# One level of Strassen's scheme in 21 of the 44 input-projection pairs of each layer, in a two-layer hybrid decoder step

## What is computed

```python
h = rms_norm(x, P['norm_mix'][l])
z = jnp.einsum('btd,dn->btn', h, P['w_in'][l])      # d = 1024, some 11300 columns
a_q, a_k, a_v, b_q, b_k, b_v, b_g, b_lr, c_qkv, c_z, c_b, c_a, gates = jnp.split(z, split_points(), axis=-1)
...
merged = (g_a * jnp.einsum('btc,cd->btd', o_a, wb[0]) + g_b * jnp.einsum('btc,cd->btd', o_b, wb[1])
          + g_c * jnp.einsum('btc,cd->btd', o_c, wb[2]))
out = jnp.einsum('btd,de->bte', merged, P['w_out'][l])
```

## Time and profile before

| | |
|---|---|
| Median of 3 runs | 1804.47 us (1804.31 to 1809.21) |
| Span of the profiled execution, first to last instruction | 1802.1 us |
| TensorE busy | 1748.8 us, 97% |
| VectorE busy | 743.5 us, 41% |
| ScalarE busy | 364.3 us, 20% |
| Mean granted TensorE clock | 0.993 |

### The profile page before, as it was taken

The page is one execution under the profiler, slowest core; times in us unless marked ns, Lnnn a source line. Parts: engine busy times, 40 slices in busy tenths (PEclk is TensorE's granted clock), DMA queues, the critical chain, the costliest instruction groups (busy, mean ns, idle before and its releaser), DMA issues.

```text
span 1802.1 us, 30183 instructions
## 1 busy us (share of the span) xinstructions
PE 1748.8 (97%) x12542; PEld 1282.9 (71%) x12542; DVE 743.5 (41%) x1548; ACT 364.3 (20%) x760; POOL 154.3 (9%) x259
## 2 busy tenths in 40 slices
PE   9999999999999999999999998999989999999997
PEld 7889888787768999978898887877663343333423
DVE  3444542434535765534544414355342332233222
ACT  2241333433101000012313333331011110100001
POOL 3000000403200111000100002032000000000000
PEclk9999999999999999999999999999999999999999
DMA  9833599999999997899535899899958999999994
GB/s 296 285 120 100 187 324 316 359 310 367 388 347 392 365 321 286 288 348 371 194 107 207 308 325 346 312 350 384 333 211 327 393 377 414 402 398 394 371 415 177
DMA packets 265853, 563.96 MB, mean 313 GB/s; under 512 B 14654, under 2 KB 163362, under 8 KB 265441
## 3 DMA queue, kind: packets, MB, share of 16 engines
q1 hardware_dynamic: 246384, 500.15, 76.8%
q0 software_dynamic: 18544, 58.58, 9.2%
q10 hardware_dynamic: 784, 3.26, 0.5%
HBM read 547.75 MB, written 196.63 MB: 413 GB/s over the span
## 4 chain that ended last, share of the span: by engine, by line
PE 85%; SPq 7%; DMA 4%; DVE 2%; issue 1%; ACT 1%; DVEq 0%; POOL 0%; ACTq 0%; POOLq 0%
PE PS L940 34%; PE PS L1598 8%; PE PS L1374 8%; SPq L811 7%; PE PS L1350 5%; PE PS L1382 4%; PE PS L859 3%; PE PS L986 3%; PE PS L1576 3%; PE PS L1364 2%; PE PS L979 2%; PE PS L1636 2%; PE PS L1321 1%; PE PS L1537 1%; DMA mem<-bias_tables 1%
## 5 line engine op out<-in xcount | busy, mean ns | idle before, releaser
L940 PE MATMUL PS<-h,mem 128*128 128x264 f32 x2816 | 654.3, 389 | 0.0
L940 PEld LDWEIGHTS PS<-h,mem 128*128 128x128 f32 x2816 | 527.8, 191 | 106.7 <-issue 21.3
L1806 ACT COPY z<-PS 128x264 f32<-128x264 f32 (+5 forms) x293 | 119.5, 430 | 737.6 <-PE PS L940 527.6
L1598 PE MATMUL PS<-mem,z 128*32 128x512 f32 (+1 forms) x1536 | 146.1, 523 | 3.8 <-DMA mem<-in_moe_w_up 3.8
L2893 DVE COPY small<-mem 128x1024 f32 x56 | 38.8, 693 | 175.6 <-PE PS L1576 117.8
L1598 PEld LDWEIGHTS PS<-mem,z 128*32 128x32 f32 x1536 | 47.4, 110 | 77.8 <-issue 61.2
L1576 PE MATMUL PS<-small,z 128*32 128x256 f32 (+2 forms) x624 | 86.9, 396 | 1.3 <-DVE z L2893 1.3
L1350 PE MATMUL PS<-z,mem 128*128 128x264 f32 x384 | 87.3, 388 | 0.0
L1576 PE MATMUL PS<-z 128*32 128x256 f32 (+2 forms) x624 | 87.0, 396 | 0.0
L1350 PEld LDWEIGHTS PS<-z,mem 128*128 128x128 f32 x384 | 72.3, 190 | 13.8 <-issue 1.7
L1374 PE MATMUL PS<-z,mem 128*128 128x132 f32 x624 | 78.3, 278 | 0.0
(11 more groups left out here) (377 smaller groups left out, 2028.2 us busy)
## 6 DMA issues: line engine op xcount, KB each, us to landing
out_win_s<-in_cache_win_kv SPq DMA_DIRECT2D x128, 1023.5 KB, 11.9
mem<-in_w_in SPq DMA_DIRECT2D x88, 1024.0 KB, 7.6
mem<-in_moe_w_gate SPq DMA_DIRECT2D x80, 512.0 KB, 9.7
mem<-in_moe_w_up SPq DMA_DIRECT2D x80, 512.0 KB, 8.9
mem<-in_moe_w_down SPq DMA_DIRECT2D x64, 512.0 KB, 13.6
out_win_s<-in_cache_win_kv SPq DMA_DIRECT2D x32, 1022.0 KB, 13.1
z<-in_moe_w_down SPq DMA_DIRECT2D x48, 512.0 KB, 13.1
z<-in_moe_w_up SPq DMA_DIRECT2D x32, 512.0 KB, 10.6
```

What stands on the lines that cost most here:

```text
L940: last = mm(bank(l, "p", j)[:, 0:T], w[:, k, P * (j % 2):P * (j % 2) + P], h[:, k, :], start=(k == 0), stop=(k == KT - 1))
L1598: last = mm(m_bank("c", "gu", g, b, w, r)[BLK * j:BLK * j + BLK, 0:n], hs[:, k, P * r + BLK * j:P * r + BLK * j + BLK], v3(slot_ap(set_slo ...
L1806: return nc.scalar.copy(out, in_)
```

## The change

For the 21 pairs of `FOLD` in each layer the two tiles are computed together by one level of Strassen's scheme. The weight chunk is split into quarters a11, a12, a21, a22 (4 blocks of 128 by 128 columns each), h into h11, h12, h21, h22 (4 blocks by 132 tokens). Seven products of four half-width matmuls take the place of sixteen matmuls: fold_x (a11 h11, and s2 by a sum of h), fold_y (s1, and a difference of weights), fold_x2 and fold_y2 (the rest, accumulated into the same banks, 0 for x and 1 for y). VectorE forms the weight sums in fold_w (four additions of 128 x 512), once a layer the sums of h in fold_h, and puts the products together: a reduction of fold_x, a reduction and an addition for fold_y, an addition for fold_y2. ScalarE copies fold_x2's half width instead of two tiles. fold_w of a pair stands in the list right behind fold_x of the pair before, where that is folded too, and else behind the first tile of the pair before. The fifth slot of the projection's ring becomes the place of the sums of h, so the ring has four slots (`RING, BASE = 4, 5`). The core of the diff:

```diff
-RING = 5
+RING, BASE = 4, 5
...
+HALF = T // 2
+UNSETTLED = ("proj", "fold_x", "fold_y", "fold_x2", "fold_y2", "fold_w")
+FOLD = (8, 9, 10, 11, *range(15, 20), *range(23, 32), 33, 35, 37)
...
+    def tile(j):
+        q = j // 2
+        if q not in FOLD:
+            return [("proj", j)]
+        return [("fold_x2", q), ("fold_y2", q)] if j % 2 else [("fold_x", q), ("fold_y", q)]
...
-    s += p() + [("small_turn",)] + p(2) + [("conv_v", 0)] + p() + [("gate_c",)] + p() + [("conv_v", 1)]
+    s += p() + [("small_turn",), ("fold_h",)] + p(2) + [("conv_v", 0)] + p() + [("gate_c",)] + p() + [("conv_v", 1)]
...
-        return [step, ("proj_half", j), (step[0] + "2", *step[1:]), ("proj", j)]
+        first, rest = tile(j) if j // 2 in FOLD else (("proj_half", j), ("proj", j))
+        return [step, first, (step[0] + "2", *step[1:]), rest]
...
+    for q in FOLD:
+        before = ("fold_x", q - 1) if q - 1 in FOLD else ("proj", 2 * q - 2)
+        s.insert(s.index(before) + 1, ("fold_w", q))
...
-        FIXED = dict(par=0, ab=1, xn=2)
+        FIXED = dict(par=0, ab=1, xn=2, fold_x=0, fold_x2=0, fold_y=1, fold_y2=1)
...
-                place(n0 + q, q % RING, (l, "p", 2 * q + 1))
+                place(n0 + q, q % RING, (l, "fold_y2", q) if q in FOLD else (l, "p", 2 * q + 1))
+            held[BASE - 1] = (l, "fold_y2", FOLD[-1])
...
+            def fold_x(l, q):
+                wait_chunk(pe, CH0[l] + q)
+                open_bank(pe, l, "fold_x", q)
+                x_ = bank(l, "fold_x", q)
+                four(x_[:, 0:HALF], fold_quarters(l, q)[0], h[:, 0:4, 0:HALF], True)
+                pe.wait_ge(hd_ready, h_sum(l, 3))
+                pe.wait_ge(fw_even, even_sum(l, q, 1))
+                four(x_[:, HALF:T], fold_sums(q)[1], fold_t[:, 1]).then_inc(full(l, "fold_x", q), 1)
+
+            def fold_y(l, q):
+                pe.wait_ge(fw_odd, odd_sum(l, q))
+                open_bank(pe, l, "fold_y", q)
+                y_ = bank(l, "fold_y", q)
+                four(y_[:, 0:HALF], fold_sums(q)[0], fold_t[:, 0], True)
+                four(y_[:, HALF:T], fold_quarters(l, q)[2], fold_t[:, 2]).then_inc(full(l, "fold_y", q), 1)
...
+            def fold_y2(l, q):
+                open_bank(pe, l, "fold_y2", q)
+                y_ = bank(l, "fold_y2", q)
+                four(y_[:, HALF:T], fold_quarters(l, q)[3], fold_t[:, 3])
+                pe.wait_ge(fw_even, even_sum(l, q, 2))
+                four(y_[:, 0:HALF], fold_sums(q)[2], h[:, 4:8, HALF:T]).then_inc(full(l, "fold_y2", q), 1)
...
+            def fold_w(l, q):
+                wait_chunk(dve, CH0[l] + q)
+                if fold_before(q) is not None:
+                    wait_full(dve, l, "fold_y2", fold_before(q))
...
+                a11, a12, a21, a22 = fold_quarters(l, q)
+                s1, s2, s4 = fold_sums(q)
+                tt(s1, a21, a22, ADD)
+                tt(a21, a11, a21, SUB).then_inc(fw_odd, 1)
+                dve.wait_ge(fw_odd, odd_sum(l, q))
+                tt(s2, a22, a21, SUB).then_inc(fw_even, 1)
+                dve.wait_ge(fw_even, even_sum(l, q, 1))
+                tt(s4, a12, s2, SUB).then_inc(fw_even, 1)
+
+            def fold_x(l, q):
+                if q != FOLD[0]:
+                    wait_read(dve, l, "fold_y2", FOLD[FOLD.index(q) - 1])
+                wait_full(dve, l, "fold_x", q)
+                nc.vector.tensor_reduce(fold_ve[:, 0, :], bank(l, "fold_x", q)[:, 0:T].rearrange("p (w t) -> p t w", w=2),
+                                        AX.X, ADD).then_inc(free(l, "fold_x", q), 1)
+
+            def fold_y(l, q):
+                wait_full(dve, l, "fold_y", q)
+                nc.vector.tensor_reduce(fold_ve[:, 1, :], bank(l, "fold_y", q)[:, 0:T].rearrange("p (w t) -> p t w", w=2),
+                                        AX.X, ADD).then_inc(free(l, "fold_y", q), 1)
+                wait_read(dve, l, "fold_x", q)
+                wait_read(dve, l, "fold_y", q)
+                tt(fold_out(q)[:, 3 * HALF:4 * HALF], fold_ve[:, 0, :], fold_ve[:, 1, :], ADD)
+
+            def fold_y2(l, q):
+                wait_full(dve, l, "fold_y2", q)
+                tt(v3(fold_out(q)[:, HALF:3 * HALF], 2), v3(bank(l, "fold_y2", q)[:, 0:T], 2),
+                   bc(fold_ve[:, 0, :], 1, [P, 2, HALF]), ADD).then_inc(free(l, "fold_y2", q), 1)
```

More of the change, by code:

```diff
@@ L136, in mixer_jobs @@
         return [("p", *a)]
+    if k in ("fold_x", "fold_y", "fold_x2", "fold_y2"):
+        return [(k, *a)]
     if k == "conv_s":
@@ L596, in wait_z @@
         def wait_z(eng, l, lo, hi):
-            for j in range(max(lo, hi - 2), hi):
+            for j in [j for j in range(lo, hi) if j // 2 not in FOLD][-2:]:
                 wait_read(eng, l, "p", j)
+            for q in [q for q in FOLD if lo <= 2 * q + 1 and 2 * q < hi][-1:]:
+                wait_read(eng, l, "fold_x2", q)
+                wait_read(eng, l, "fold_y2", q)
         CH0 = [0, CH_MIX + CH_FFG + CH_FFD]
@@ L950, in proj, with four, fold_x2 @@
                 proj_ks(l, j, range(4, KT) if (l, j) in halved else range(KT))
+            def four(out, left, right, opens=False):
+                for k in range(4):
+                    last = mm(out, left[:, k, :], right[:, k, :], start=(opens and k == 0), stop=(k == 3), skip_group_check=True)
+                return last
+            def fold_x(l, q):
[12 more added lines that the diff above has]
+                four(y_[:, HALF:T], fold_quarters(l, q)[2], fold_t[:, 2]).then_inc(full(l, "fold_y", q), 1)
+            def fold_x2(l, q):
+                open_bank(pe, l, "fold_x2", q)
+                four(bank(l, "fold_x2", q)[:, 0:HALF], fold_quarters(l, q)[1], h[:, 4:8, 0:HALF]).then_inc(
+                    full(l, "fold_x2", q), 1)
+            def fold_y2(l, q):
[4 more added lines that the diff above has]
+                four(y_[:, 0:HALF], fold_sums(q)[2], h[:, 4:8, HALF:T]).then_inc(full(l, "fold_y2", q), 1)
             def conv_s(l):
@@ L1843, in proj, with fold_x2 @@
                 copy(z[:, j, :], bank(l, "p", j)[:, 0:T]).then_inc(free(l, "p", j), 1)
+            def fold_x2(l, q):
+                wait_full(act, l, "fold_x2", q)
+                copy(fold_out(q)[:, 0:HALF], bank(l, "fold_x2", q)[:, 0:HALF]).then_inc(free(l, "fold_x2", q), 1)
             def small_turn(l):
@@ L2060, in _ @@
                     if step[0] in run:
-                        if step[0] != "proj":
+                        if step[0] not in UNSETTLED:
                             settle()
@@ L2966, in _ @@
             link(nc.vector.memset(cba, 0.0))
-            run = dict(small=small_step, small_turn=small_turn, conv_v=conv_v, conv_s=conv_s, conv_t=conv_t, conv_a=conv_a,
+            run = dict(small=small_step, small_turn=small_turn, fold_h=fold_h, fold_w=fold_w, fold_x=fold_x, fold_y=fold_y,
+                       fold_y2=fold_y2, conv_v=conv_v, conv_s=conv_s, conv_t=conv_t, conv_a=conv_a,
                        cz=cz, gate_c=gate_c, norm_sum=norm_sum, gdn_dec=gdn_dec, gdn_a=gdn_a, gdn_inv=gdn_inv,
```

92 lines of the change are left out of this document (66 added, 26 removed).

## The result

The changed kernel takes 1848.6 us (median of four runs, 1845.0 to 1850.8) against 1804.4: **1.024 times the kernel before, 95% interval 1.0217 to 1.0264**. The profiled execution has a span of 1848.7 us, 46.6 more than the 1802.1 of before. The change loses 44 us where 38 of matmul work were meant to go.

The account below looks back on a forecast made before the run. The prediction took TensorE, busy for 97% of the span, as the bound. It summed 1804.5 + 14.2 (waits less matmul savings) + 10.1 (ring of four) + 3.4 (clock) = 1832 us, with a range of 1796 to 1852.

Parts of the forecast that it names:

- The sign: Whole kernel: slower than before, given a chance of 0.75, against 0.17 for faster and 0.08 for the same.
- the ring of four: Projection loads with one slot less: delays at layer 0's chunk 5 and feed-forward start, together +10.1 us.
- The gain of a pair: TensorE, each folded pair: 6.22 us instead of 7.12, 0.90 saved; 37.8 us over 42 pairs.
- The waits: TensorE waiting for VectorE around folded pairs: 26.0 us a layer against 18.9 saved, +14.2 over two layers.
- Pairs 28 to 30: Norm stretch: VectorE's multiplication and weight sums delay fold_y2, 2.5 us a pair, 7.5 in all.
- gs_a: State step after pairs 16 to 19: needs two VectorE copies that stand behind pair 19's end, 1.8 us.
- Chunk 5: Layer 0's first pairs: the chunk is issued at the end of pair 1 and lands late, 2.5 us, bounds 0 and 3.4.
- The start of the feed-forward stage: Layer 0 behind w_out: turned slots make the second feed-forward chunk land late, 7.6 us, bounds 6 and 14.
- The clock: New TensorE waits bring two spells of half clock, +3.4 us; bounds 0 and ten spells (+17).
- in most of a layer one pair less costs nothing: Ring loads: three folded pairs are still 18.7 us, for a landing that takes 7.8 in the median; cost 0.
- (a): Rival: fold_y2 finds its bank free, mixers cover the sums everywhere but at pairs 8 and 15; 1790 us, chance 0.15.
- (c): Rival: waits as walked, clock falls at ten of them, layer 1's first loads come late; 1854 us, chance 0.18.

Follow-up runs that it names:

- ring_alone: Changed kernel with the ring of four and turned slots kept, but only pair 37 of the 21 folded pairs still folded: 1825.9 us.
- sums_late: Changed kernel with only VectorE's order changed: the next pair's weight sums stand behind both reductions of the pair before: 1830.4 us.
- copies_alone: Changed kernel with only the background copies of the cache moved, to chunks 20 to 44: 1833.7 us.
- late_five_copies: Changed kernel with weight sums behind both reductions, five slots where sums of h don't live, pair 15 plain, cache copies moved to earlier chunks: 1811.4 us.
- no_15: Changed kernel with pair 15 alone made plain again: 1839.9 us.

## Why the prediction was right, and where not

The sign holds, and so does the main reason given for it: fold_w between the two reductions, and its place behind the inversion, take more than the matmuls give. But half of the loss, the 22 us of ring_alone, is the ring of four, for which the prediction had 10.1. The time, 1848.6, lies in the range, 17 us above the forecast and 3 below the range's end. Term by term:

- **The gain of a pair** was put at 0.90; it is 8.90 - 8.19 = 0.71, by sums_late's norm stretch, where nothing waits. A pair takes 8.19 - 1.78 = 6.41, not 6.22: the issues come every 0.1125 us (2.70 for 24), which makes 6.30, and the first issue of fold_x2 takes twice as long (306.31 to 307.32 for eight is 1.01, not 0.90). 42 x 0.71 = 29.8 instead of 37.8.
- **The waits** were walked to 26.0 a layer; the gaps of layer 1 are at the places named, and most are smaller. Pairs 28 to 30: 1.8 each, 5.5 (7.5 forecast), the norm step every 10.28 (10.5 forecast, though its terms add up to 10.41). Pair 31: 1.1 (1.4). Pair 8: 1.8 (2.7). Pairs 9 to 11 and the tile after: 2.4 (4.0). Pair 15: 4.0, and 3.7 in layer 0 (3.8). Pairs 16 to 19: none (1.3). gs_a: 1.4 and 0.5 behind it (1.8). Pairs 23 to 27: 1.1 (2.6). Pair 33: 1.3, in layer 0 only (0.9). That is 18.9 in layer 0 and 17.8 in layer 1, 36.7 where 52 were forecast. These 15 us and the 8 by which the gain of the pairs fell short have separate reasons, and offset each other in part.
- **Chunk 5**: 2.1 us of wait (2.5). **The start of the feed-forward stage**: 9.8 (7.6, bounds 6 and 14). The prediction followed the second chunk, and that is the one whose wait ends last. It was issued at 581.14 and its first sum started at 588.10: 7.0 us to landing, where the prediction took the shortest load, 4.8, and these 2.2 are what the term was short of. VectorE waits longer for the first chunk, 9.0 us, but was through with it at 585.6. Some of the work behind the gaps ran at half clock.
- **The clock**: two spells were forecast. In the projections four stand behind waits (at 63.7, 155.9, 309.5 and 944.4, each 3.41 us at 0.50), TensorE busy for 13.2 of their 13.6 us, so 6.6 us lost against 3.4. There is also the one at the feed-forward's start, where the kernel before has 3.41 us; of it the view by window says:

```profile
585.95:599.60 13.65, 6.36 (x21) 4.89 (x22) 8.59 (x17) 2.66 (x5) 0.00 (x0) 0.50 1.05 399
```

- **The step that failed** is the sentence that "in most of a layer one pair less costs nothing". It looked at TensorE's wait for its own chunks, for which it holds outside layer 0's start. It did not look at what the shifted loads and copies meet on the DMA queues: the loads of cached values in the attention of the sample tokens. That cost 4.3 and 5.4 us in the one step, which is over half of the 7.6 and 8.1 us by which the two attention stages came out above the forecast. ring_alone has the wait without the folds, copies_alone takes it away without touching the ring.

Put together: -29.8 + 36.7 (waits) + 2.1 + 9.8 + 9.8 (cached values) + 6.6 = 35.2 of the 46.6 us. Of the other 11, up to 1.7 are a spell of 3.41 us at half clock at 446.0, in the attention of layer 0, where the kernel before has none, and 2.4 are longer waits of TensorE for VectorE's additions to the attention's scores (10.6 us over both layers, 8.2 before). The other 7 are spread; part of them is that a pair with a wait takes longer than its wait (the norm step 10.28 where 8.19 and 1.83 make 10.02). No run separates them.

That the time lies in the range is partly luck: the waits were put 15 us too high, and this covered most of the 21 us (cached values and the 11 that are not in the sum above) for which the prediction had no term.

The sums of the changed kernel take 0.68 to 0.69 us each and start 0.60 to 0.72 apart, as in the earlier trace rows, so the trace's price was the right one for the walk. The table in the Trainium skill, "VectorE: DVE Perf Modes", section on the TRN2 errata, makes a sum of 512 columns an estimated 594 ns. The prediction stopped at the table: right below it the same section says that this row is too low, and gives (N + 151) / 0.96 for an fp32 addition, 691 ns at 512. With that the trace agrees.

Of the rivals, (a), that the mixers cover the sums, is out: the gaps stand where the order puts them. In sums_late fold_y2 does find its bank free at pairs 8 and 28 to 30, but the time there is 1830.4 and not 1790. (c) came closest in time, 1854, by its own mechanism in part (more spells of half clock), not by late loads in layer 1's first pairs, of which the trace has none.

## What to carry to other kernels

A change that saves 0.7 us a pair on the bounding engine can't afford waits of 0.9 us a pair (36.7 over 42 pairs): look at which bank or buffer the bounding engine needs next, and put the helper engine's long work behind the operation that frees it, not ahead. That was worth 18 us with not one instruction more or less. A buffer taken from a prefetch ring is paid for not only where the ring runs short of chunks; follow every load and background copy that shifts by one slot to what it meets at its new place. And after such a change ask of each of its parts whether it pays for itself: 12 us came out of 18 pairs a layer, where 20 in the first order had lost 23.

## What the runs showed of the hardware that was not expected

Where background copies of 1 MB stand beside smaller transfers, these come several microseconds later: VectorE waited 5.2 us for the inverses from DRAM in late_five_copies, and the step over cached values takes 5.4 and 6.6 us less in copies_alone than in the changed kernel. Issuing can itself hold a queue: two copies took SP 7.76 us to issue in one trace and 1.20 in another. Where they took over 7 us, the step over cached values was the shorter one in all such runs; no run changes this alone. And a spell of 3.41 us at half clock stands at the end of, or right behind, four of the changed kernel's waits in the projections (2.1, 3.7, 1.8 and 4.0 us), each up to 1.7 us on top; behind the five other waits of 1.8 in the norm stretches there is none. In no_15 a wait of 2.3 us at chunk 5 has none either, so the length of the wait alone doesn't decide it.
